# Token halves in alternating order over the products and weight tiles of a two-layer encoder step

## The chip, the cores and the metric

The kernel runs on one core of one Trainium2 chip. The metric is the device time of one execution in microseconds (us), as the median of several runs. Engines are TensorE (PE, with its weight loads PEld), VectorE (DVE), ScalarE (ACT), GpSimd (POOL) and SyncE (SP).

## What is computed

One inference step of an encoder with two layers, for 512 prompt tokens and 64 sample tokens that share all weights, so 576 token columns in all. D_MODEL is 1024, the FFN width 2752. Per layer:

```python
hp = post_add(hp, swiglu(pre_mod(hp, g[0], mp[0], mp[1]), ffn_w1[l, 0], ffn_w2[l, 0]), g[1], mp[2], FFN_RES)
yp, st_p = mixer_prompt(pre_mod(hp, g[2], mp[3], mp[4]), *mw)
hp = post_add(hp, yp, g[3], mp[5], 1.0)
hp = post_add(hp, swiglu(pre_mod(hp, g[4], mp[6], mp[7]), ffn_w1[l, 1], ffn_w2[l, 1]), g[5], mp[8], FFN_RES)
```

and the same for the sample. `pre_mod` is an RMS norm with scale and shift, `post_add` a gated residual. The mixer projects x with one wide `w_in` into the q, k, v of two kinds of attention (4 and 8 heads of 64), a spatial gating branch and three gates, multiplies each branch by its gate and goes through `w_out`. Everything is float32.

## The kernel before, in words

Tokens lie along the free dimension (576 columns), features on the 128 partitions. A dense product is made of weight tiles of 128 x 128. Each weight and each activation is split into a high and a low part of type float32r, and a product is taken as three: w_hi by x_hi, w_hi by x_lo, w_lo by x_hi, all accumulated in PSUM. A matmul covers one half of the tokens: half 0 has 288 columns, half 1 has 288 in the stages that use `columns(b)`, and 290 in those that use `moving(b)` (two more columns carry the shift). So a weight tile costs six matmuls: three products by two halves. Each half has a PSUM bank of its own, `ps[:, 2 * out + b]`, and `out` picks one of the pairs of banks in turn, so that VectorE and ScalarE empty one pair while TensorE fills another. Every matmul loads its weights anew.

`split_tile` (line 660) issues these six. The order of the halves is set on line 666: in the stages with `columns` product 1 takes the halves the other way round (01 10 01); in the stages with `moving` every product takes half 0 first (01 01 01). Line 668 is the matmul, and all its callers show as that line in the trace.

Who calls it: `whole_chunk` (689) takes a chunk of eight weight tiles (one DMA of 512 KB), for the first FFN products ("f1", moving), the gates (moving) and the first five chunks of the output product ("out", columns). `ffn` (821) takes the second FFN products ("f2", columns) output by output, 22 weight tiles each; the last of them (`tail_tile`, 672) has only w_hi and w_lo by hid_hi and an order of its own, which stays. `project_tile` and `project_more` (909, 920) take moving tiles, mostly one or two at a time between the small matmuls of the attention. `third_gate` (1103) and `merge` (1112) make the gates (moving) and the branches (columns, chunks split in 2, 4 and 2 tiles). Three places take one half at a time and pass it as `halves=(b,)`: `first_group` (724, moving), the last output of f2 (856) and the last three chunks of out (882). There the order of halves means nothing.

In each layer the order is: ffn a, projections and attention, merge, output product, ffn b. The semaphore of a chunk is counted up by the last matmul of its last tile. VectorE makes w_lo from the loaded weights and w_hi (line 1553), ScalarE makes w_hi (line 1162), SyncE's queue loads chunks five slots ahead.

Of the kernel before, what the change touches and what calls it, by code (L numbers as in the profile page):

```python
# [299 lines left out]
def build_program(nc, ins, outs):  # L300
# [355 lines left out]
    def _(pe):  # L656
# [3 lines left out]
        def split_tile(out, c, t, hi, lo, cols, first, last, halves=BOTH):  # L660

            s = c % SLOTS
            wh, wl = w_hi[:, s, t * P:(t + 1) * P], w_lo[:, s, t * P:(t + 1) * P]
            for n, (w, xx) in enumerate(((wh, hi), (wh, lo), (wl, hi))):

                for b in halves[::-1] if cols is columns and n == 1 else halves:
                    width = cols(b).stop - cols(b).start
                    r = mm(ps[:, 2 * out + b, 0:width], w, xx[:, cols(b)],  # L668
                           start=first and n == 0, stop=last and n == 2)
            return r  # L670
# [18 lines left out]
        def whole_chunk(l, ph, i, p, group, hi, lo, cols, gate=None):  # L689

            c = chunk(l, ph, i)
            chunk_ready(c)
            pair_free(l, ph, p, group)
            for t in range(KD):
                if gate is not None:
                    gate(t)
                r = split_tile(p, c, t, hi[:, t, :], lo[:, t, :], cols, t == 0, t == KD - 1)
            r.then_inc(chunk_done.sem, 1)

        def x_half(l, ph, s, k, b):  # L700

            return split_tile(s, chunk(l, ph, s), k, x_hi[:, k, :], x_lo[:, k, :], moving, k == 0, k == KD - 1, (b,))
# [118 lines left out]
        def ffn(l, ab, n):  # L821
# [16 lines left out]
            for o in range(KD - 1):  # L838
                pair_free(l, ph, o % 2, o // 2)
                for t in f2_tiles(o):  # L840
                    c, k = chunk(l, ph, t // CHUNK_TILES), t - o * KF
                    if t % CHUNK_TILES == 0 or k == 0:
                        chunk_ready(c)
                    if o == 0:
                        pe.wait_ge(prod_lo.sem, prod_lo.done(l, at + k))
                    if k < KF - 1:
                        r = split_tile(o % 2, c, t % CHUNK_TILES, hid_hi[:, k, :], hid_lo[:, k, :], columns,
                                       k == 0, False)
                    else:
                        r = tail_tile(o % 2, c, t % CHUNK_TILES, BOTH)  # L850
                    if t % CHUNK_TILES == CHUNK_TILES - 1:
                        r.then_inc(chunk_done.sem, 1)
                    elif k == KF - 1:
                        r.then_inc(f2_done.sem, 1)
                ada_work(l, ab, F1_SLOTS + o)
# [1517 lines left out]
```

## Time and profile before

| | us |
|---|---|
| median of 3 runs | 2849.2 (2848.51 to 2849.84) |
| the profiled execution, its own time | 2847.8 |
| its span, first to last instruction | 2846.0 |
| TensorE busy, matmuls | 2783.9 (98%) |
| TensorE busy, weight loads | 2628.9 (92%) |
| VectorE busy | 1298.3 (46%) |
| ScalarE busy | 971.0 (34%) |

Mean granted TensorE clock: 0.997 of full speed. The end of a matmul's record is modelled, and successive matmuls overlap in the records; so the pace of a stretch is read from the starts of its rows, not from their durations. The timeline joins neighbouring instructions of one line and the same operands into a row: "x2" is the pair of matmuls of one product, and its shape is that of the first of them.

### The profile page before, as it was taken

The numbers are of one execution on the slowest core, as the hardware profiler recorded it, in microseconds if no ns is written. First come the engines' busy times: TensorE is split into PE (matmuls) and PEld (weight loads), VectorE is DVE, ScalarE is ACT, GpSimd is POOL, SyncE is SP. The second block draws the span as 40 slices with busy tenths as digits, with TensorE's granted clock in tenths as the row PEclk, the third lists the DMA queues.
The fourth block names the chain that finished last, engine by engine and source line by source line (L and its number), as shares of the span: only waits on it lengthen the run. The fifth ranks groups of instructions, "written<-read, shape, count | busy, mean of one in ns | idle before, by whom it ended". The sixth has DMA issues, their size and how long they took to land.

```text
span 2846.0 us, 49978 instructions
## 1 busy us (share of the span) xinstructions
PE 2783.9 (98%) x21654; PEld 2628.9 (92%) x21654; DVE 1298.3 (46%) x2533; ACT 971.0 (34%) x1821; POOL 111.2 (4%) x210
## 2 busy tenths in 40 slices
PE   7999999999999999999999999999999999999997
PEld 6999999878999989999999999998889999999997
DVE  3444424655544464443264443256555445544423
ACT  4222324444422452222252222244443225422322
POOL 0000000010000000000000000001100000000000
PEclk9999999999999999999999999999999999999999
DMA  6444532333222234432224444323322222222221
GB/s 245 149 148 149 172 121 93 110 123 98 92 82 82 82 104 149 148 134 88 88 86 152 149 149 165 112 100 116 122 96 68 82 82 75 82 82 82 86 87 66
DMA packets 90186, 319.82 MB, mean 112 GB/s; under 512 B 11360, under 2 KB 14464, under 8 KB 89776
## 3 DMA queue, kind: packets, MB, share of 16 engines
q1 hardware_dynamic: 64048, 222.50, 23.4%
q0 software_dynamic: 25920, 94.14, 9.7%
q8 instruction: 171, 2.80, 0.4%
q14 instruction: 47, 0.39, 0.0%
HBM read 305.70 MB, written 11.55 MB: 111 GB/s over the span
## 4 chain that ended last, share of the span: by engine, by line
PE 85%; DVE 7%; ACT 3%; DVEq 2%; issue 2%; DMA 1%; SPq 0%; ACTq 0%
PE ps L668 77%; PE ps L782 2%; PE ps L1013 2%; PE ps L1059 1%; DVE h L1671 1%; ACT w_hi L1162 1%; DVE x_lo L1678 1%; PE ps L1035 1%; DVEq L1670 1%; DVE z L1669 1%; PE ps L677 1%; DMA w_raw<-in_f 1%; ACT sig L1498 1%; ACT x_hi L1254 1%; DVEq L2017 1%
## 5 line engine op out<-in xcount | busy, mean ns | idle before, releaser
L668 PE MATMUL ps<-x_hi,w_hi 128*128 128x290 f32 (+1 forms) x4256 | 973.8, 304 | 22.7 <-DVE x_lo L1678 13.6
L668 PE MATMUL ps<-x_lo,w_hi 128*128 128x290 f32 (+1 forms) x4256 | 935.4, 295 | 0.0
L668 PE MATMUL ps<-x_hi,w_lo 128*128 128x290 f32 (+1 forms) x4256 | 934.8, 295 | 0.0
L668 PEld LDWEIGHTS ps<-x_hi,w_hi 128*128 128x128 f32 x4256 | 686.7, 189 | 95.1 <-issue 65.3
L668 PEld LDWEIGHTS ps<-x_lo,w_hi 128*128 128x128 f32 x4256 | 701.1, 190 | 0.3
L668 PEld LDWEIGHTS ps<-x_hi,w_lo 128*128 128x128 f32 x4256 | 692.7, 189 | 0.0
L1553 DVE TENSOR_TENSOR w_lo<-w_raw,w_hi 128x1024 fp32r<-128x1024 f32 x386 | 468.8, 1222 | 254.2 <-ACT w_hi L1162 251.9
L1162 ACT CAST w_hi<-w_raw 128x1024 fp32r<-128x1024 f32 x386 | 392.9, 1047 | 77.3 <-DMA w_raw<-in_f 77.3
L668 PE MATMUL ps<-hid_hi,w_hi 128*128 128x288 f32 x1344 | 300.8, 295 | 1.8 <-DVE c_col L1610 1.8
L668 PE MATMUL ps<-hid_hi,w_lo 128*128 128x288 f32 x1344 | 300.7, 295 | 0.0
L668 PE MATMUL ps<-hid_lo,w_hi 128*128 128x288 f32 x1344 | 298.7, 293 | 0.0
L1192 ACT CAST hid_hi<-hid 128x576 fp32r<-128x576 f32 x84 | 56.6, 673 | 497.5 <-DVE hid L1582 497.5
L668 PEld LDWEIGHTS ps<-hid_hi,w_hi 128*128 128x128 f32 x1344 | 219.3, 188 | 6.6 <-issue 3.3
L668 PEld LDWEIGHTS ps<-hid_lo,w_hi 128*128 128x128 f32 x1344 | 218.5, 188 | 0.2
L668 PEld LDWEIGHTS ps<-hid_hi,w_lo 128*128 128x128 f32 x1344 | 218.4, 188 | 0.0
L1609 DVE TENSOR_TENSOR hid<-ps,r 128x576 f32<-128x576 f32 x80 | 60.6, 757 | 331.2 <-PE ps L668 331.2
L1188 ACT ACTIVATE sil<-sil,c_col 128x512 f32<-128x512 f32 (+1 forms) x168 | 80.9, 529 | 278.3 <-DVE c_col L1610 267.3
L1625 DVE TENSOR_TENSOR acc_y<-acc_y,sq 128x576 f32<-128x576 f32 (+1 forms) x52 | 33.4, 641 | 279.3 <-ACT sq L1232 252.2
L1609 DVE TENSOR_TENSOR sil<-ps,r 128x576 f32<-128x576 f32 x76 | 57.5, 757 | 175.8 <-PE ps L668 175.8
L1232 ACT ACTIVATE sq<-ps 128x576 f32<-128x576 f32 x38 | 24.8, 651 | 296.4 <-PE ps L677 263.1
L2150 POOL DMA_DIRECT2D ada_w<-in_ada x128 | 67.6, 532 | 1407.4 <-PE ps L782 1364.4
L1498 ACT ACTIVATE sig<-sig,c_col 128x512 f32<-128x512 f32 x96 | 46.0, 528 | 188.1 <-DVE c_col L2080 188.1
(214 smaller groups left out, 2391.8 us busy)
## 6 DMA issues: line engine op xcount, KB each, us to landing
w_raw<-in_f SPq DMA_DIRECT2D x260, 512.0 KB, 3.5
ada_w<-in_ada POOLq DMA_DIRECT2D x128, 512.0 KB, 5.7
w_raw<-in_gate SPq DMA_DIRECT2D x64, 512.0 KB, 3.5
w_raw<-in_tri SPq DMA_DIRECT2D x42, 512.0 KB, 3.5
ada_first<-in_ada SPq DMA_DIRECT2D x4, 2048.0 KB, 17.7
w_raw<-in_wout SPq DMA_DIRECT2D x16, 512.0 KB, 3.4
decay_s<-f_scratch POOLq DMA_DIRECT2D x16, 272.0 KB, 6.0
decay_p<-f_scratch POOLq DMA_DIRECT2D x8, 512.0 KB, 5.9
```

The source lines that it names most:

```text
L668: r = mm(ps[:, 2 * out + b, 0:width], w, xx[:, cols(b)], start=first and n == 0, stop=last and n == 2)
L677: r = mm(ps[:, 2 * out + b, 0:HALF], w[:, s, t * P:(t + 1) * P], hid_hi[:, k, columns(b)], start=False, stop=w is w_lo)
L782: r = mm(out[32 * j:32 * j + 32, :], cond_s[:, 2 * k:2 * k + 32], w[:, j * ADA_COLS:(j + 1) * ADA_COLS], start=k == 0, stop=k == KD - 1)
L1013: r = mm(out, q_st[rows, i * P:i * P + m], k, start=True, stop=True)
L1162: copy(w_hi[:, c % SLOTS, :], w_in[:, c % SLOTS, :]).then_inc(hi_ready.sem, 1)
L1188: r = A(sil[:, i, part], sil[:, i, part], ACT.Silu, bias=c_col[:, 2 * (i % 2), g:g + 1])
L1192: copy(hid_hi[:, i, :], hid[:, i, :]).then_inc(prod_hi.sem, 1)
L1498: r = A(sig[:, br, part], sig[:, br, part], ACT.Sigmoid, bias=c_col[:, br, g:g + 1])
L1553: V.tensor_tensor(w_lo[:, s, :], w_in[:, s, :], w_hi[:, s, :], ALU.subtract).then_inc(lo_ready.sem, 1)
L1609: V.tensor_tensor(two(dst), pair[p], two(r2[:, :]), ALU.mult)
L1625: V.tensor_tensor(total, total, more, ALU.add).then_inc(y_added.sem, 1)
L2150: nc.gpsimd.dma_start(dst, src).then_inc(signal.sem, 16)
```

## The change

Line 666 is the only one that changes. The order now depends on the product n and on the weight tile's number t in its chunk, in all stages: for even t 01 10 01, for odd t 10 01 10. A tile ends with the half with which the next one begins.

```diff
             for n, (w, xx) in enumerate(((wh, hi), (wh, lo), (wl, hi))):
 
-                for b in halves[::-1] if cols is columns and n == 1 else halves:
+                for b in halves[::-1] if (n + t) % 2 else halves:
                     width = cols(b).stop - cols(b).start
                     r = mm(ps[:, 2 * out + b, 0:width], w, xx[:, cols(b)],
                            start=first and n == 0, stop=last and n == 2)
```

## Rows read from the trace of the kernel before

**Rows 1.** The page: busy time and instructions, granted clock by slice, the chain.

```profile
PE 2783.9 (98%) x21654; PEld 2628.9 (92%) x21654; DVE 1298.3 (46%) x2533; ACT 971.0 (34%) x1821; POOL 111.2 (4%) x210
...
PEclk9999999999999999999999999999999999999999
...
PE 85%; DVE 7%; ACT 3%; DVEq 2%; issue 2%; DMA 1%; SPq 0%; ACTq 0%
PE ps L668 77%; PE ps L782 2%; PE ps L1013 2%; PE ps L1059 1%; DVE h L1671 1%; ACT w_hi L1162 1%; DVE x_lo L1678 1%; PE ps L1035 1%; DVEq L1670 1%; DVE z L1669 1%; PE ps L677 1%; DMA w_raw<-in_f 1%; ACT sig L1498 1%; ACT x_hi L1254 1%; DVEq L2017 1%
```

**Rows 2.** TensorE's waits: us in total, times, longest us.

```profile
PE ps L668 <- DVE x_lo L1678: 13.6, 23, 3.6
...
PE ps L668 <- DVE c_col L1610: 9.7, 17, 1.0
```

**Rows 3.** Groups of TensorE by shape: count, busy us, mean ns, idle before.

```profile
L668 PE MATMUL ps<-x_hi,w_hi 128*128 128x288 f32 x2128 | 660.2, 310 | 17.1 <-DVE x_lo L1678 8.8 <-DVE c_col L1610 7.8 <-ACT hid L1209 0.5
L668 PE MATMUL ps<-x_hi,w_hi 128*128 128x290 f32 x2128 | 635.0, 298 | 5.6 <-DVE x_lo L1678 4.9 <-DVEq L2124 0.7
...
L668 PE MATMUL ps<-hid_hi,w_hi 128*128 128x288 f32 x1344 | 300.8, 295 | 1.8 <-DVE c_col L1610 1.8
...
L668 PE MATMUL ps<-m_hi,w_hi 128*128 128x288 f32 x256 | 62.7, 296 | 0.0
...
L668 PE MATMUL ps<-o_hi,w_hi 128*128 128x288 f32 x256 | 56.2, 301 | 1.4
```

**Rows 4.** Timeline, moving, both halves: start us, us, instruction.

```profile
1288.84 0.43 PE L668 MATMUL ps<-x_hi,w_hi 128*128 128x288 f32 x2
1289.11 0.43 PE L668 MATMUL ps<-x_lo,w_hi 128*128 128x288 f32 x2
1289.37 0.43 PE L668 MATMUL ps<-x_hi,w_lo 128*128 128x288 f32 x2
...
1292.04 0.30 PE L668 MATMUL ps<-x_hi,w_hi 128*128 128x288 f32 x1
```

**Rows 5.** Timeline, columns, both halves, upper level.

```profile
1317.34 0.42 PE L668 MATMUL ps<-hid_hi,w_hi 128*128 128x288 f32 x2
...
1333.14 0.42 PE L668 MATMUL ps<-hid_hi,w_hi 128*128 128x288 f32 x2
```

**Rows 6.** Timeline, columns, both halves, lower level.

```profile
372.11 0.42 PE L668 MATMUL ps<-hid_hi,w_hi 128*128 128x288 f32 x2
...
386.93 0.42 PE L668 MATMUL ps<-hid_hi,w_hi 128*128 128x288 f32 x2
```

**Rows 7.** Timeline, columns, half 0 alone, then half 1 alone.

```profile
2811.36 0.29 PE L668 MATMUL ps<-hid_hi,w_hi 128*128 128x288 f32 x1
...
2821.47 0.29 PE L668 MATMUL ps<-hid_hi,w_lo 128*128 128x288 f32 x1
...
2822.49 0.29 PE L668 MATMUL ps<-hid_hi,w_hi 128*128 128x288 f32 x1
...
2828.67 0.30 PE L668 MATMUL ps<-hid_hi,w_lo 128*128 128x288 f32 x1
```

**Rows 8.** Timeline, moving, one half alone: half 0, half 1, half 0.

```profile
1442.25 0.29 PE L668 MATMUL ps<-x_hi,w_hi 128*128 128x288 f32 x1
...
1445.32 0.29 PE L668 MATMUL ps<-x_hi,w_lo 128*128 128x288 f32 x1
...
1904.57 0.29 PE L668 MATMUL ps<-x_lo,w_hi 128*128 128x290 f32 x1
...
1905.79 0.29 PE L668 MATMUL ps<-x_lo,w_hi 128*128 128x290 f32 x1
...
1909.14 0.30 PE L668 MATMUL ps<-x_hi,w_lo 128*128 128x290 f32 x1
...
2405.99 0.29 PE L668 MATMUL ps<-x_hi,w_hi 128*128 128x288 f32 x1
...
2409.42 0.29 PE L668 MATMUL ps<-x_hi,w_lo 128*128 128x288 f32 x1
```

## Prediction: what the new order does to the pace

> **What bounds the kernel now.** I read the page first. TensorE is busy for 98% of the span, its weight loads (which lie beside its matmuls) for 92%, and the granted clock is at nine tenths of full speed or more in every slice, so the upper level of 2.4 GHz nearly throughout; the chain that ended last is 85% TensorE, 77% of it line 668, the one line that the change reorders [rows 1]. The list of TensorE's waits says the same from the other side: the two largest for this line add up to 13.6 + 9.7 us in a span of 2846.0 us [rows 2]. No DMA and no other engine paces the long stages. So a change of order is worth what it does to the pace, the time from the start of one matmul of line 668 to the start of the next, and nearly all of it reaches the end.
>
> **How many matmuls.** The list of groups by shape has 2128 matmuls of 288 columns and 2128 of 290 for each of the three products over x, 1344 per product over hid, 256 over m and 256 over o [rows 3]. Of the moving ones, 3 x 8 x 6 = 144 per shape and product belong to first groups, which take one half at a time and keep their order. So 1984 moving weight tiles take both halves (six matmuls each, 11904 in all); by the code 2 x 141 of these are scattered between the attention's small matmuls, the other 1702 run in unbroken rows. Tiles of columns that take both halves: 28 x 21 = 588 in the second FFN products, 2 x 5 x 8 = 80 in the output product, 2 x 8 x 8 = 128 in the branches, 796 in all.
>
> **The paces before**, each from the starts of a first and a last row of the timeline.
> - Moving, both halves, order 01 01 01: 12 rows of two matmuls take 1292.04 - 1288.84 = 3.20 us, so 133.3 ns each at a mean of 289 columns [rows 4]. The same figure stands in long stretches of the first FFN products and of the gates.
> - Columns, both halves, order 01 10 01: 1333.14 - 1317.34 = 15.80 us for 20 tiles of six, so 131.7 ns at 288 columns [rows 5]. Another stretch of the same stage and order runs 386.93 - 372.11 = 14.82 us for 19 tiles, 130.0 ns [rows 6]. So one order, one width and one kind of tile can run at either of two levels; read in the same way, 6 of the 28 outputs of the second FFN products run at the lower one, the others at the upper.
> - Columns, one half at a time: half 0, 2821.47 - 2811.36 = 10.11 us for 76 starts, 133.0 ns; half 1, 2828.67 - 2822.49 = 6.18 us for 47 starts, 131.5 ns; mean 132.3 [rows 7].
> - Moving, one half at a time: half 0 at 288 columns, 3.43 us for 26 starts (131.9 ns) in one stretch and 3.07 us for 23 (133.5 ns) in another, mean 132.7; half 1 at 290 columns, 4.57 us for 34 starts, 134.4 ns; mean of both halves 133.6 [rows 8].
>
> **The change part by part.** Nothing is added or removed: the same 3 x 6112 = 18336 pairs of weight load and matmul, the same semaphores, and the increment still sits on the last matmul of a tile. Three things move.
> (1) In a moving tile the seams between products 0 and 1 and between 1 and 2 now repeat a half (and so a PSUM bank) instead of changing it: 2 x 1984 = 3968 seams.
> (2) From one weight tile to the next of a row the half is repeated too, in moving stages (up to 7 seams per 8 tiles, 1736) and in columns (20 per output of the second FFN product, 7 per output chunk, 5 per branch chunk: 560 + 70 + 80 = 710).
> (3) In odd moving tiles, and odd column tiles, half 1 opens and half 0 closes. A chunk therefore ends with half 0. Its readers wait for the increment on the last matmul and read both banks, and the next chunk writes another pair of banks, so no engine gets work earlier or later than the pace itself makes it. I cost this at nothing; what covers it is that the other waits of the line are short [rows 2].
>
> The price of a repeated half is not in the trace by itself for moving tiles; the nearest rows are the three orders above. Repeated halves throughout (one half at a time) cost 132.3 ns in columns, the mixed order there 131.7: the mixed one is 0.6 ns better. In moving tiles repetition throughout costs 133.6, alternation throughout 133.3: 0.3 better. If the mixed order is as good against repetition in moving tiles as in columns, it gives 133.6 - 0.6 = 133.0, and taking the lower level of columns into the mean, (22 x 131.7 + 6 x 130.0) / 28 = 131.3, it gives 133.6 - 1.0 = 132.6. Against 133.3 that is 0.3 to 0.7 ns; with the faster of the two stretches of half 0 the base falls by 0.4 and the gain is up to 1.1. I take 0.65, near the middle of these ends: 11904 x 0.65 = 7.7 us. The bounds: everything to the lower level that columns reach, plus the width, gives at best 133.3 - (130.0 + 1.0) = 2.3 ns, 27 us; the slower side is the third case. For (2) in columns I take nothing: the ends are the pace of 130.0 in all 4776 matmuls (from a mean of 131.4: -7 us) and half way to 132.3 (+2 us).
>
> At one place the skill speaks against all this. The trace has 133.3 and 131.7 ns where 288 columns at 2.4 GHz take 120 [rows 4, 5], and the surplus differs with order [rows 7]. The Trainium skill ("TensorE: Matmul & The Clock Gate", Part 2, on loading the weights) says that the next weights come through a read port of their own and take no bandwidth from the running matmul, and its section "Back-to-back issue gap" makes the isolated gap N / 2.4 + 2.5 ns whatever the order: 122.5 ns here. By that rule no order can matter, and the change is worth 0 us. The trace does not agree on the size of the gap; whether it agrees on the order is what is asked.
>
> **The rivals.**
> *A, the forecast: the mixed order is slightly better in moving tiles too.* For it: columns, where mixed beats repeated by 0.6 to 2.3 ns with equal operands [rows 5 to 7]. Against it: part of the 1.6 ns between columns and moving tiles is width and row layout, since one half at a time shows 132.3 against 133.6 as well [rows 7, 8]. Time: 2847.8 - 7.7 = 2840.1 us for the profiled execution.
> *B, the order is of no account and 133.3 is what 289 columns cost.* For it: the difference between stages at equal order (1.3 ns, from rows 7 and 8) nearly covers the difference between the two-half stretches (1.6 ns). The pace of moving tiles is the same in every long stretch, whatever other engines do. Time: 2847.8 us, at most 3 us to either side.
> *C, slower: a half that is read again at once costs.* Half 1 of x at 290 columns is the slowest thing in the trace: 134.4 ns over the stretch and 135.6 in its first part (1905.79 - 1904.57 = 1.22 us for 9) [rows 8]. The snake puts each 290-column matmul next to another one at every seam between products. If pairs of 290 run at 135.6 and pairs of 288 at 133.0, the mean is 134.3, 1.0 ns more than now: 11904 x 1.0 = +11.9 us, and 1 to 2 us in columns: 2847.8 + 13 = 2860.8 us. It decides as soon as a moving tile of six takes more than 800 + 5.7 / 1984, that is 802.9 ns.
> That the change does nothing at all because the engine reorders is part of B: matmuls of this line start in program order in the trace.
>
> **How the numbers follow.** The profiled execution has a span of 2846.0 us and a time of 2847.8, the median of the three runs is 2849.2, so 1.4 us are added: A 2841.5, B 2849.2, C 2862.2. A measurement of this kernel can tell about 0.2%, 5.7 us, from no change. A's own range is 2822 to 2846 (2.3 ns at the far end, 0.3 at the near). Chances: A 0.43, of which its weakest sizes fall within 0.2% and are counted as such (0.03); B 0.35, C 0.22, of which 0.01 is within 0.2%. So faster 0.40, same 0.39, slower 0.21. The predicted time is A's, 2841.5. The range has to reach B and most of C: 2827 to 2861 leaves out A's lowest level and C's worst.
>
> **What would show it.** In the timeline of the changed kernel, rows of moving tiles should open with a 290-column matmul at every second product, which shows the order itself. Then the 12 rows that take 3.20 us now: under A 3.17 to 3.19, under B 3.20, under C 3.22 or more. The stretches of columns show by themselves what the seam between tiles is worth (15.80 us for 20 tiles now). The busy time of the other engines, the waits for x_lo and c_col and the clock should stand as they are; if the time moves while the pace does not, my reading is wrong, and it is wrong as well if the pace moves by another level (1.6 ns or more), since I take levels as rare.

## The result and the profile after

The changed kernel takes 2864.45 us (median of 4 runs, 2862.89 to 2865.27) against 2848.86 us for the kernel before: a ratio of 1.0054, 95% interval 1.0038 to 1.0070. It is slower by 15.6 us, where I had forecast 7.7 us less, and it lies beyond the end of my range (2861). The profiled execution took 2865.1 us with a span of 2863.3, that is 17.3 us more than the span before.

The page of the changed kernel, busy time, granted clock and chain:

```profile
PE 2802.4 (98%) x21654; PEld 2647.7 (92%) x21654; DVE 1299.0 (45%) x2533; ACT 971.2 (34%) x1821; POOL 111.2 (4%) x210
...
PEclk9999999999999999999999999999999999999999
...
PE 88%; DVE 6%; ACT 2%; DVEq 2%; issue 1%; DMA 1%; SPq 0%; ACTq 0%
PE ps L668 80%; PE ps L782 2%; PE ps L1013 2%; PE ps L1059 1%; DVE h L1671 1%; DVE x_lo L1678 1%; PE ps L1035 1%; DVEq L1670 1%; DVE z L1669 1%; PE ps L677 1%; DMA w_raw<-in_f 1%; DVEq L2017 1%; ACT x_hi L1254 0%; ACT w_hi L1162 0%; DVE w_lo L1553 0%
```

and its two largest waits of line 668:

```profile
PE ps L668 <- DVE x_lo L1678: 13.6, 23, 3.6
...
PE ps L668 <- DVE c_col L1610: 9.6, 17, 1.0
```

TensorE's busy time is up by 18.5 us (2783.9 before) and the share of line 668 in the chain from 77 to 80%, while the clock and the waits stand as in [rows 1, 2]. The time went into the pace of line 668 and nowhere else. Moving tiles in a stretch of a first FFN product of the changed kernel (the columns are start us, us, instruction):

```profile
76.07 0.43 PE L668 MATMUL ps<-x_hi,w_lo 128*128 128x288 f32 x2
76.34 0.43 PE L668 MATMUL ps<-x_hi,w_hi 128*128 128x290 f32 x2
76.60 0.43 PE L668 MATMUL ps<-x_lo,w_hi 128*128 128x288 f32 x2
...
87.58 0.43 PE L668 MATMUL ps<-x_hi,w_hi 128*128 128x290 f32 x2
```

The rows open with 288 and 290 columns in turn, so the order is what it should be. From the first 290-column opening of a tile, at 76.34, to the last, at 87.58, there are 14 tiles: 11.24 us / 84 = 133.8 ns, against 133.3 in [rows 4]. Columns, an output of a second FFN product:

```profile
1324.55 0.43 PE L668 MATMUL ps<-hid_hi,w_hi 128*128 128x288 f32 x2
...
1340.68 0.42 PE L668 MATMUL ps<-hid_hi,w_hi 128*128 128x288 f32 x2
```

20 tiles take 16.13 us, 134.4 ns each, against 131.7 and 130.0 in [rows 5, 6].

Over all unbroken stretches of a trace (at least seven matmuls in a row, starts less than 0.18 us apart; 10624 gaps of moving tiles, some 3500 in the second FFN products) the mean paces went from 133.27 to 133.66 ns in moving tiles and from 131.37 to 134.30 in the second FFN products, from 131.66 to 134.29 in the output product and from 132.13 to 133.96 in the branches. 11904 x 0.39 = 4.6 us, 3528 x 2.93 = 10.3, 480 x 2.63 = 1.3, 768 x 1.83 = 1.4: together 17.6 us, where the span grew by 17.3. Output by output, the second FFN products ran at two levels before, 6 of the 28 outputs at 130.1 ns and 22 at 131.7 to 131.8; in the changed kernel all 28 run at 134.2 to 134.4. Three quarters of the loss is in the stages with columns, where the change adds only 710 of its 6414 repeated halves. (A "repeated half" is the same half of the columns twice running. In this change it is never the same data: it is x_hi and then x_lo, or the other way round, or one row of activations and then the next.)

### The profile page after: what moved, and what is told of

Read it like the earlier page. It is cut to its first block, busy times and chain, and to the rows that moved or that the text cites. A ratio compares the mean times of both kernels' runs of the same rounds, so it can differ in the third digit from the quotient of the medians.

```text
span 2863.3 us, 49978 instructions
## 1 busy us (share of the span) xinstructions
PE 2802.4 (98%) x21654; PEld 2647.7 (92%) x21654; DVE 1299.0 (45%) x2533; ACT 971.2 (34%) x1821; POOL 111.2 (4%) x210
## 4 chain that ended last, share of the span: by engine, by line
PE 88%; DVE 6%; ACT 2%; DVEq 2%; issue 1%; DMA 1%; SPq 0%; ACTq 0%
PE ps L668 80%; PE ps L782 2%; PE ps L1013 2%; PE ps L1059 1%; DVE h L1671 1%; DVE x_lo L1678 1%; PE ps L1035 1%; DVEq L1670 1%; DVE z L1669 1%; PE ps L677 1%; DMA w_raw<-in_f 1%; DVEq L2017 1%; ACT x_hi L1254 0%; ACT w_hi L1162 0%; DVE w_lo L1553 0%
## 5 line engine op out<-in xcount | busy, mean ns | idle before, releaser
L668 PE MATMUL ps<-x_hi,w_hi 128*128 128x288 f32 (+1 forms) x4256 | 966.8, 303 | 22.6 <-DVE x_lo L1678 13.6
L668 PE MATMUL ps<-x_lo,w_hi 128*128 128x288 f32 (+1 forms) x4256 | 944.6, 298 | 0.0
L668 PE MATMUL ps<-x_hi,w_lo 128*128 128x288 f32 (+1 forms) x4256 | 937.0, 296 | 0.0
L668 PEld LDWEIGHTS ps<-x_hi,w_lo 128*128 128x128 f32 x4256 | 701.4, 190 | 0.0
L668 PEld LDWEIGHTS ps<-x_lo,w_hi 128*128 128x128 f32 x4256 | 693.1, 189 | 0.3
## 6 DMA issues: line engine op xcount, KB each, us to landing
ada_first<-in_ada SPq DMA_DIRECT2D x4, 2048.0 KB, 17.6
```

Source lines behind the costliest of these rows:

```text
L668: r = mm(ps[:, 2 * out + b, 0:width], w, xx[:, cols(b)], start=first and n == 0, stop=last and n == 2)
```

## The experiments

All diffs are against the kernel before and concern line 666 unless they say otherwise. Paces are the means just described, from one profiled execution of each kernel. "Columns" in a pace means the second FFN products: the mean over their 28 outputs that take both halves. Where outputs of one kernel run at different levels, such a mean is a mixture, and the text says so. "Snake" is the new order, "inner turn" the 01 10 01 inside a tile.

**First set: which part, which stage.**

1. The new order in columns alone.

```diff
-                for b in halves[::-1] if cols is columns and n == 1 else halves:
+                for b in halves[::-1] if ((n + t) % 2 if cols is columns else False) else halves:
```

> The new order in the stages with columns alone; moving stages as before. Theory S (the seam from tile to tile): the paces of the two traces add up, columns 131.4 -> 134.2 ns for 4776 matmuls, so +13.5 us against before, near 2862.5, and moving tiles stay at 133.3. Theory R (every repeated half costs the same, in any stage): half of the 6414 new repeated halves' price would be missing; only 710 of them are in columns, so +2 us at most, near 2851.

Measured: 2860.48 us against 2849.18, ratio 1.0040 (1.0025 to 1.0055); columns 134.21 ns (26 outputs at 134.2 to 134.4, two at 133.3 to 133.4), moving 133.28.

2. The new order in moving stages alone.

```diff
+                for b in halves[::-1] if (n == 1 if cols is columns else (n + t) % 2) else halves:
```

> The new order in the moving stages alone; columns as before. Theory S: +4 to +5 us (133.27 -> 133.66 ns for 11904 matmuls), near 2853.5, columns back at 131.4 with six outputs at 130.0. Theory R: +13 to +15 us, near 2863.

Measured: 2852.9 us, ratio 1.0013 (1.0004 to 1.0022); moving 133.52, columns 131.60. The two parts give +11.3 and +3.7 us, together 15.0 of the 15.6: they add up, and theory R, a fixed price for each repeated half, is out. In columns 2 of the 28 outputs run at 130.1 here, where it was 6 in the kernel before, though their order is the same: the mixture of levels can change by 0.2 ns without any edit to the stage.

3. The inner turn in every stage, no turn from tile to tile.

```diff
+                for b in halves[::-1] if n == 1 else halves:
```

> 01 10 01 in every tile of every stage: columns as before, moving tiles turn the order inside the tile but not from tile to tile. Theory S: moving tiles keep 133.3 ns or gain a little (my forecast's mechanism gave 132.6 to 133.0), since only the seam between tiles hurts: 2841 to 2850. Theory R: 3968 of the 5704 repeated halves of the moving stages stay, so +3 us against before or more, 2852 to 2858.

Measured: 2846.86 us, ratio 0.9992 (0.9982 to 1.0001). Moving tiles run at 132.95 ns; in the timeline of this kernel

```profile
244.19 0.42 PE L668 MATMUL ps<-x_hi,w_hi 128*128 128x288 f32 x2
...
255.35 0.43 PE L668 MATMUL ps<-x_hi,w_hi 128*128 128x288 f32 x2
```

14 tiles take 11.16 us, 132.9 ns. So part (1) of the change comes out at the pace that I forecast for it (133.0 ns), though the gain in time is within the noise; it is part (2), the seam from tile to tile, laid over it, that turns it into a loss (133.5 to 133.7 with both).

4. Pure alternation in every stage.

```diff
+                for b in halves:
```

> 01 01 01 in every tile of every stage: moving tiles as before, columns lose their inner turn and have no repeated half at all. Theory S: the seam from tile to tile stays the half 1 -> half 0 of the next row, so columns keep 131 to 132 ns, total within 3 us of before. Theory R: no repeated half is best, columns at 130 to 131 ns, -2 to -6 us. The third case, that columns need just the inner turn: 132.5 ns or more, +5 us.

Measured: 2854.36 us, ratio 1.0017 (1.0008 to 1.0027). In columns,

```profile
1321.28 0.43 PE L668 MATMUL ps<-hid_hi,w_hi 128*128 128x288 f32 x2
...
1335.68 0.43 PE L668 MATMUL ps<-hid_hi,w_hi 128*128 128x288 f32 x2
```

18 tiles take 14.40 us: 133.3 ns, the pace that moving tiles have with this order, at one column less. Over all of the second FFN products the mean is 132.83, since in the first FFN of each layer the last two of the seven outputs with both halves fall to 130.0. So the third case holds: in columns the inner turn is worth 1.2 to 1.5 ns of the mean. The result had already ruled out the first half of my rival B, that order is of no account; this rules out the second, that 133.3 is what 289 columns cost: it stands at 288 as well.

**Second set: what about the seam between tiles.**

5. In columns every tile begins with half 1.

```diff
+                for b in halves[::-1] if cols is columns and n != 1 else halves:
```

> In columns every tile is 10 01 10: the inner turns stay, the seam between tiles changes half (0 -> 1) and never repeats one, but it is no longer half 1 -> half 0 of the next row, which lies right behind it in memory. Moving as before. If a repeated half (bank or read) at the tile seam is the cost: columns at 131.6 ns, total within 2 us of before. If the cost is that the read no longer runs on from row to row: columns at 133.5 to 134.2 ns, +10 to +12 us.

Measured: 2851.47 us against 2848.98, ratio 1.0010 (1.0000 to 1.0019); columns 132.14. It lies between my two answers, and the mean is a mixture: 21 of the 28 outputs run at 131.6 to 131.8 as before, the other 7 at 133.3. So a read that runs on from one row into the next is not needed for 131.7, and it is not what makes the slow order slow.

6 and 7. Reads in one order, PSUM banks in the other. The diff is that of 6; 7 has `zip(was, snake if cols is columns else halves)`.

```diff
-                for b in halves[::-1] if cols is columns and n == 1 else halves:
+                was = halves[::-1] if cols is columns and n == 1 else halves
+                snake = halves[::-1] if cols is columns and (n + t) % 2 else halves
+                for b, bank in zip(snake if cols is columns else halves, was):
                     width = cols(b).stop - cols(b).start
-                    r = mm(ps[:, 2 * out + b, 0:width], w, xx[:, cols(b)],
+                    r = mm(ps[:, 2 * out + bank, 0:width], w, xx[:, cols(b)],
```

> In columns the halves are read in the new order, but each matmul writes the PSUM bank that stood at its place in the old order, so the sums of the two halves are mixed up there and the output is another. Moving as before. If the repeated PSUM bank costs: 131.6 ns, total near 2849. If the order of reads costs: 134.1 ns as in the new order in columns alone, near 2860.5.

> The reverse: in columns the halves are read in the old order and the banks are written in the new one; the output is another. Moving as before. If the bank costs: 134.1 ns, near 2860.5. If the reads cost: 131.6 ns, near 2849.

Measured: 2860.02 us (ratio 1.0040, 1.0025 to 1.0055) and 2849.35 us (1.0001, 0.9992 to 1.0011) against 2848.98; columns 134.25 and 131.52 ns. In the timeline, reads in the new order (line 670 here is the matmul):

```profile
1322.48 0.43 PE L670 MATMUL ps<-hid_hi,w_hi 128*128 128x288 f32 x2
...
1337.80 0.42 PE L670 MATMUL ps<-hid_hi,w_hi 128*128 128x288 f32 x2
```

and reads in the old one, from three outputs that follow each other:

```profile
1301.03 0.43 PE L670 MATMUL ps<-hid_hi,w_hi 128*128 128x288 f32 x2
...
1316.35 0.43 PE L670 MATMUL ps<-hid_hi,w_hi 128*128 128x288 f32 x2
...
1317.69 0.42 PE L670 MATMUL ps<-hid_hi,w_hi 128*128 128x288 f32 x2
...
1333.30 0.42 PE L670 MATMUL ps<-hid_hi,w_hi 128*128 128x288 f32 x2
...
1334.60 0.42 PE L670 MATMUL ps<-hid_hi,w_hi 128*128 128x288 f32 x2
...
1341.71 0.42 PE L670 MATMUL ps<-hid_hi,w_hi 128*128 128x288 f32 x2
```

With the new order of reads 19 tiles in 15.32 us are 134.4 ns. With the old one the first of the three outputs runs just as slowly (19 tiles in 15.32 us), the second at 130.1 ns (20 tiles in 15.61 us) and the third at 131.7 (9 tiles in 7.11 us). The slow one is the only one of the 28 in experiment 7, and in the other traces no output with the old order of reads is as slow; why this one is, no run shows. On the whole kernel the order of the banks has no price that can be told from noise (0.4 us in experiment 7, -0.5 us between experiments 1 and 6). The price of the change in columns, 11.0 us at equal banks (2860.02 against 2848.98), goes with the order in which the halves are read from SBUF.

8. In columns the order turns from tile to tile only.

```diff
+                for b in halves[::-1] if cols is columns and t % 2 else halves:
```

> In columns 01 01 01 and 10 10 10 in turn: no turn inside a tile, a repeated half only at the seam between tiles. Moving as before. The inner turn was worth 133.3 - 131.6 = 1.7 ns against pure alternation. If the seam between tiles costs 2.5 ns a matmul whatever the inside: 135 ns or more, near 2866. If only the mixture of inner turns and tile turn falls out of step: 133 to 133.5 ns, near 2855 as with alternation.

Measured: 2850.23 us against 2848.98, ratio 1.0006 (0.9996 to 1.0015); columns 131.76 ns. This was neither of my two answers, and it is the most telling run: without the inner turn, a repeated half at the seam between tiles costs nothing. Against pure alternation it gains nearly as much as the inner turn. Of the orders tried, those with both together are slow.

9. The inner turn in every tile of columns, and every other seam between tiles repeats a half.

```diff
+                for b in halves[::-1] if cols is columns and (n + (t + 1) // 2) % 2 else halves:
```

> In columns the inner turns stay in every tile, and every other seam between tiles repeats a half (t = 0 to 1, 2 to 3 and so on), the rest change it. Moving as before. If each repeated tile seam has a price: half of 2.5 ns, columns at 132.9 ns, near 2855. If only the unbroken series 0 1 1 0 0 1 1 0 falls out of step: 132 ns or less, within 2 us of before.

Measured: 2854.85 us against 2849.69, ratio 1.0019 (1.0010 to 1.0028); columns 132.96, with all outputs between 132.6 and 133.3. Half of the seams cost about half of the price, so it is not the unbroken series alone.

**Third set: where the reads lie.** Experiments 11, 13 and 14 have line 666 as in experiment 1 and the edit shown besides.

10. The snake in columns with the parts of even and odd tiles exchanged.

```diff
+                for b in halves[::-1] if cols is columns and (n + t) % 2 == 0 else halves:
```

> The unbroken snake in columns with its phase turned: even tiles 10 01 10, odd tiles 01 10 01, so each half meets the other rows' addresses. Moving as before. If the price hangs on the unbroken series: 134.1 ns again, near 2860.5. If it hangs on which half is read at which address: another pace, by 0.5 ns or more.

11. The snake in columns, with hid, o and m 128 bytes further on.

```diff
-    big = (arena[0] + ALIGN - 1) // ALIGN * ALIGN
+    big = (arena[0] + ALIGN - 1) // ALIGN * ALIGN + 128
```

> The snake in columns as in the first experiment, with hid, o and m (and all that lies behind them) 128 bytes further on in SBUF; x and the weights stay. If the price hangs on the relative position of activations and weights in SBUF: a pace other than 134.1 ns by 0.5 or more, the time nearer to 2849 or beyond 2863. If it hangs on the order alone: 134.1 ns, near 2860.5.

13. The snake in columns, odd tiles reading the row before theirs (the same edit in all five calls with columns).

```diff
-                        r = split_tile(o % 2, c, t % CHUNK_TILES, hid_hi[:, k, :], hid_lo[:, k, :], columns,
+                        r = split_tile(o % 2, c, t % CHUNK_TILES, hid_hi[:, k - k % 2, :], hid_lo[:, k - k % 2, :], columns,
```

> The snake in columns, and in all stages with columns a tile of odd number reads the activation row before it, so the rows start at the same place within 512 bytes throughout (two rows are 4608 bytes apart). The output is another. Moving as before. If the price needs the step of 2304 bytes from row to row: columns at 131.7 ns or less, near 2849. If it comes from the order of halves alone: 133.5 to 134.1, near 2860.

14. The snake in columns, one weight tile for all eight.

```diff
-            wh, wl = w_hi[:, s, t * P:(t + 1) * P], w_lo[:, s, t * P:(t + 1) * P]
+            at = 0 if cols is columns else t * P
+            wh, wl = w_hi[:, s, at:at + P], w_lo[:, s, at:at + P]
```

> The snake in columns, and in all stages with columns the first weight tile of the chunk is used for all eight, so the place that weights are read from changes only between high and low part. The output is another. Moving as before. If the price needs the walk through the weight tiles: 131.7 ns, near 2849. If not: 134.1, near 2860.

Measured, in this order: 2859.0 and 2859.5 us against 2849.69, 2860.12 and 2859.66 us against 2849.31 (ratios 1.0034, 1.0036, 1.0038 and 1.0037, each to within 0.0015), columns at 133.80, 134.12, 134.21 and 134.17 ns. None of the four takes the price away, so it needs neither this position of the activations, nor the step from row to row, nor the walk through the weights. Other distances, such as that between the two halves of a row, were not tried. The exchange of even and odd tiles moves the mean most, by 0.4 ns: 13 of the 28 outputs run at 133.3 there, against two or three in experiments 1, 11, 13 and 14.

**Fourth set: a better order.**

12. Moving stages turn from tile to tile only, columns as before.

```diff
+                for b in halves[::-1] if (n == 1 if cols is columns else t % 2) else halves:
```

> In moving stages 01 01 01 and 10 10 10 in turn; columns as before. In columns this order was as good as the inner turn (131.7 against 131.6, alternation 133.3). If moving tiles answer as columns do: 133.0 ns as with the inner turn, near 2847. If the repeated seam between tiles costs in them by itself: 133.5 or more, near 2852.

Measured: 2844.4 us against 2849.69, ratio 0.9981 (0.9971 to 0.9991). Moving tiles run at 132.74 ns; at the end of a first FFN product

```profile
1265.49 0.43 PE L668 MATMUL ps<-x_hi,w_hi 128*128 128x290 f32 x2
...
1294.96 0.43 PE L668 MATMUL ps<-x_hi,w_hi 128*128 128x288 f32 x2
```

37 tiles take 29.47 us, 132.7 ns for each matmul. That is better than either of my answers.

15. The same turn in all stages.

```diff
+                for b in halves[::-1] if t % 2 else halves:
```

> 01 01 01 and 10 10 10 in turn in all stages. If the two edits add up (columns alone +1.3, moving alone -5): near 2845.5, moving at 132.7 ns, columns at 131.7.

Measured: 2843.97 us against 2849.31, ratio 0.9982 (0.9973 to 0.9991); moving 132.74, columns 131.74. The two edits add up, as expected.

16. Moving tiles all 10 01 10, columns as before.

```diff
+                for b in halves[::-1] if (n == 1 if cols is columns else n != 1) else halves:
```

> Moving tiles all 10 01 10, columns as before: inner turns without a repeated half between tiles, as in the products-only kernel but with the halves exchanged. If only the kind of seams counts: 133.0 ns, near 2847. If it counts which half is doubled (four half-1 reads of 290 columns have a 290 neighbour, as before): 133.5, near 2852.

Measured: 2849.91 us, ratio 1.0003 (0.9993 to 1.0012); moving 133.33 ns. The inner turn gains 0.3 ns with half 0 first and nothing with half 1 first, as columns lost 0.5 ns in experiment 5. The expectation gave a wrong picture of which reads have a neighbour of 290 columns: both orders double one half 0 and one half 1 in each tile. So it isn't the width that makes this difference, and what does is open.

The paces by order, in ns, with the share of seams that repeat a half:

| order (tile, next tile) | share | columns | the 28 outputs of columns | moving |
|---|---|---|---|---|
| 01 01 01, same | 0 | 132.83 | 4 at 130.0, 24 at 133.3 | 133.27 |
| 01 01 01, 10 10 10 | 1/6 | 131.7 to 131.8 | all at 131.7 to 132.0 | 132.74 |
| 01 10 01, same | 1/3 | 131.4 to 131.6 | 2 to 6 at 130.1, nearly all others at 131.7, one at 134.4 (experiment 7) | 132.95 |
| 10 01 10, same | 1/3 | 132.14 | 21 at 131.7, 7 at 133.3 | 133.33 |
| 01 10 01 and every other tile seam | 5/12 | 132.96 | all at 132.6 to 133.3 | not run |
| 01 10 01, 10 01 10 (the change) | 1/2 | 134.2 to 134.3 | 26 to 28 at 134.2 to 134.4 | 133.5 to 133.7 |
| one half at a time | 1 | 132.6 | other outputs: half 0 at 133.3, half 1 mostly at 131.7 | 132.6 (288), 134.5 (290) |

## Why the prediction was wrong

**What bounds the kernel** held: line 668 is the chain, waits and clock did not move, and the differences in pace times the counts give 17.6 us against the 17.3 by which the span grew. So did the counts of tiles and seams.

**Part (1), the turn inside a moving tile**, held in its pace: 132.95 ns measured where I had 132.6 to 133.0. That the figure came out is at least in part luck. The base, one half at a time, is itself a mean of two levels in columns, 133.3 and 131.7, and I misread its first half: the 76 starts from 2811.36 to 2821.47 in [rows 7] are 62 gaps of half 0, then the tail tile and 12 matmuls of half 1. Half 0 by itself runs at 133.3 ns, so the mean is 132.4 or 132.5 and not 132.3. My 0.65 ns was twice what came, 0.32, so the term would have been 3.8 us instead of 7.7; the run itself shows 2.3 us, not clear of noise.

**Part (2), the seam from tile to tile, is the step that failed.** I wrote "For (2) in columns I take nothing", with ends of -7 and +2 us, and in the moving stages I gave it no price of its own: I took one discount of "the mixed order" for (1) and (2) together. Laid over the inner turn, it costs 11.3 us in columns (experiment 1) and about 6 us in moving stages (2852.9 against 2846.86 in experiments 2 and 3). The bound of +2 us came from interpolation: a share of 1/2 should have lain between the mixed order at 1/3 and one half at a time at 1. The table shows that there is no such line. The snake is slower than both its neighbours, and two edits of which each gains 1.1 to 1.5 ns on the mean of pure alternation in columns (132.83) lose 1.4 ns when one is laid over the other. I had also written that my reading is wrong if the pace moves by another level, "since I take levels as rare". Columns moved by 2.9 ns, and the levels are not rare: 6 of 28 outputs were at another one before, and four of the six orders of the table that mix the halves show two.

**Part (3)** held as far as the list of waits shows: the waits of line 668 add up to what they were.

**The rivals.** C had the sign, and its 2862.2 us is only 2.3 us below the result, but that is luck: its mechanism is not what happened. It put 11.9 us into moving tiles, by pairs of 290 columns, and 1 to 2 us into columns; it was 4.6 us in moving tiles and 13.0 in columns, at 288 columns, so the width is not what it takes. B fell with the result and with experiment 4. The rule of the Trainium skill ("TensorE: Matmul & The Clock Gate", Part 2), that the next weights take no bandwidth from the running matmul, made the change worth 0; experiment 6 speaks against the use I made of it: with the same number of instructions and the weights, banks and widths of the kernel before, the order of the reads is worth 11.0 us. It does not show whether it is the weight load that these reads meet. The 122.5 ns beside it is a figure for an isolated matmul, as the prediction says; every pace here is that of an unbroken stream, so the 130 to 134 ns are no test of it.

**What stays open** is why. One and the same series of reads runs at 130.0 ns in one output and at 131.7 in another [rows 5, 6], so the order of the reads does not fix the pace by itself. The single starts, which the trace holds to the nanosecond, show what a level is: a pattern of gaps that repeats. In experiment 4 the outputs at 133.3 ns go 131, 131, 132, 140 over and over, with a long gap at every fourth matmul, and the four outputs at 130.0 go 129, 131 or 128, 132. A tile has six matmuls, so the long gap falls into product 0, 1 and 2 equally often: it is not tied to one seam of the tile. The two outputs at 133.3 to 133.4 in experiment 1, with the snake, also have a long gap, of 139 or 140, at every fourth matmul. So like patterns arise under different orders. It may be that an order decides which patterns can hold and how often each is met; that was not tested, nor what starts one.

The load of the other engines and of DMA does not sort the levels in the kernel before. Five windows of 16 us in outputs of the second FFN products (the columns are the window, its length, busy us of PE, PEld, DVE, ACT and POOL, the clock, the DMA share and GB/s):

```profile
334.80:350.80 16.00, 16.00 (x125) 16.00 (x125) 6.25 (x12) 5.43 (x7) 0.90 (x2) 1.00 0.57 183
371.50:387.50 16.00, 16.00 (x125) 16.00 (x125) 3.92 (x5) 3.33 (x5) 0.72 (x2) 1.00 0.41 133
389.60:405.60 16.00, 16.00 (x123) 16.00 (x123) 3.85 (x4) 3.34 (x5) 0.74 (x2) 1.00 0.41 138
1300.60:1316.60 16.00, 16.00 (x125) 16.00 (x125) 5.90 (x11) 5.43 (x7) 0.00 (x0) 1.00 0.39 118
1334.50:1350.50 16.00, 16.00 (x123) 16.00 (x123) 4.43 (x5) 4.52 (x7) 0.00 (x0) 1.00 0.20 69
```

The first, second and fourth are at 130.1 ns (125 matmuls), the third and fifth at 131.8 (123). The second and third carry nearly the same load, and the fifth, with the least DMA, is one of the slow ones.

Two things were not tried. One is whether the weight loads have part in it, since each matmul needs one. The other is pure alternation that begins with half 1 (10 10 10), which would tell whether the change from half 0 to half 1 is cheaper than the change back. If each kind of seam had a price of its own, the means of experiments 1, 4, 5 and 8 and of the kernel before would need that order to run at some 126 ns (my estimate), below everything in any trace here; so such prices are unlikely, but not excluded by a run.

## What to carry to other kernels

For the back-to-back matmuls of this kernel a fixed price per repeated half is the wrong model: two orders that each gain lose when combined, and the pace of an order could not be interpolated from its neighbours. Where TensorE is the bound and the stream is regular, the order of the moving reads can be worth measuring: here it made between 0.2% less and 0.5% more, and it costs a one-line run. Run each part of such an edit alone before both together, and look at the stretches one by one before you trust a mean pace. In this kernel a turn once per weight tile, in all stages, is as good as any order tried, 5.3 us (0.18%) below the kernel before; with the turn in the moving stages alone it is the same.

## What the runs showed of the hardware

The start-to-start pace of 288-column float32r matmuls with a weight load each, at a mean granted clock of 0.997, moves with the order in which the moving operand's two halves are read, but is not fixed by it: 130.0, 131.7, 133.3 and 134.2 to 134.4 ns were all held over 18 tiles or more. The first three recur in several kernels, about 1.7 ns apart, and one program changes between them from one output to the next. At 133.3 ns (experiment 4) the gaps repeat with a period of four matmuls, 131, 131, 132, 140 ns. Which PSUM bank a matmul accumulates into, the same as the last one's or the other, made no difference to the mean (131.5 against 131.4 ns, and 134.25 against 134.21 with the snake). Neither a shift of the activations by 128 bytes nor a fixed weight tile took the slow order below 134.1 ns in the mean (134.12 and 134.17).
